# Moving the sample steps, the LayerNorm centring and the last output scaling between slots and engines of a hybrid decoder step

## What is computed

```python
# one layer; x is the residual stream, 1024 wide; 2048 prompt tokens and 16 sample tokens per core
x += 0.5 * swiglu_1(rms(x))
u, v, q, k, vB, gB, lr, gateA, gateB = split(rms(x) @ w_in)
v_n = layernorm(gelu(v)) * ln_g + ln_b                # mixer A: spatial gating in chunks of 128
y_A = gelu(u) * (tril(W_s[g]) @ v_n + b_s[g])
S_t = diag(a_t) S_{t-1} + k_t^T v_t;  o_t = q_t S_t   # mixer B: gated linear attention, 4 heads
y_B = rms_head(o) * silu(gB)
x += (sigmoid(gateA) * (y_A @ Wa) + sigmoid(gateB) * (y_B @ Wb)) @ w_out
x += 0.5 * swiglu_2(rms(x))
x += (p @ w_ple) * sigmoid(rms(x) @ w_ple_gate)
y = x * g_final * rsqrt(mean(x*x) + eps)
# every sample token owns a state S (4 x 128 x 256) that it reads, updates once and writes back
```

## Time and profile before

| | |
|---|---|
| time, median of 3 runs | 1668.87 us (1667.63 to 1670.02) |
| profiled execution, its own time | 1666.47 us |
| its span on the slowest core (core 0) | 1664.9 us |
| spans of the 8 cores | 1655.2 to 1664.9 us |
| PE busy on core 0 | 1593.3 us, 96% of the span |
| DVE, ACT, POOL busy | 676.5, 514.4, 153.5 us |

### The profile page before, as it was taken

How to read it: one execution, slowest core, us unless ns; L and a number is a source line. 1 busy time by engine, 2 the same in 40 slices (tenths; PEclk the granted TensorE clock), 3 DMA queues, 4 the chain that set the end, 5 groups by cost and what they waited for, 6 DMA issues and landing times.

```text
span 1664.9 us, 22936 instructions; the slowest of 8 cores (1655.2 to 1664.9 us)
## 1 busy us (share of the span) xinstructions
PE 1593.3 (96%) x9276; PEld 876.5 (53%) x9276; DVE 676.5 (41%) x1220; ACT 514.4 (31%) x996; POOL 153.5 (9%) x171
## 2 busy tenths in 40 slices
PE   5999999788999999999999999999999999999995
PEld 2555544344455545544666665555566666666652
DVE  3212247548445221366422225664624542222366
ACT  3112135543323112236111213575321331111144
POOL 3001000000000000000010000000000000000027
PEclk8999999889999999999999999999999999999998
DMA  9996361867746457368654424236325335325303
GB/s 161 137 158 111 41 105 32 165 162 165 153 69 97 74 78 107 62 122 127 141 82 65 70 40 68 46 46 120 52 41 87 51 51 95 58 45 84 64 1 114
DMA packets 144169, 147.74 MB, mean 89 GB/s; under 512 B 4064, under 2 KB 140016, under 8 KB 144064
## 3 DMA queue, kind: packets, MB, share of 16 engines
q0 software_dynamic: 115936, 112.01, 45.0%
q1 hardware_dynamic: 28128, 34.27, 6.8%
HBM read 240.07 MB, written 17.40 MB: 155 GB/s over the span
## 4 chain that ended last, share of the span: by engine, by line
PE 87%; DVE 4%; ACT 3%; issue 3%; DMA 2%; DVEq 0%; ACTq 0%; SPq 0%; POOLq 0%
PE ps L512 60%; PE ps L593 18%; PE ps L613 2%; PE ps L731 2%; DVE s_tsg L1677 1%; DMA s_ring<-w_ffn_in 1%; PE ps L474 1%; DMA s_ring<-w_in 1%; DVE s_xn L1315 1%; DMA s_zone<-xT 1%; PE ps L533 1%; ACT s_Sb L1164 1%; DVE s_zone L1680 1%; PE ps L760 1%; DVE s_Sf L1455 1%
## 5 line engine op out<-in xcount | busy, mean ns | idle before, releaser
L512 PE MATMUL ps<-s_xn,s_ring 128*128 128x384 bf16 (+2 forms) x5216 | 936.6, 338 | 5.4 <-ACT s_tsg L1072 1.9
L512 PEld LDWEIGHTS ps<-s_xn,s_ring 128*128 128x128 bf16 x5216 | 509.2, 98 | 405.7 <-issue 4.7
L1362 DVE TENSOR_TENSOR s_zone<-s_tsg,ps 128x384 bf16<-128x384 f32 (+2 forms) x220 | 127.8, 584 | 451.3 <-PE ps L512 431.4
L593 PE MATMUL ps<-s_zone,s_ring 128*128 128x384 bf16 (+2 forms) x1760 | 308.9, 338 | 0.0
L1050 ACT ACTIVATE s_tsg<-ps 128x384 f32<-128x384 f32 (+2 forms) x220 | 112.4, 514 | 475.3 <-PE ps L512 460.5
L593 PEld LDWEIGHTS ps<-s_zone,s_ring 128*128 128x128 bf16 x1760 | 172.2, 98 | 134.7
L1004 ACT ACTIVATE s_sqr<-s_zone 128x384 bf16<-128x384 f32 (+2 forms) x163 | 86.8, 547 | 293.2 <-DVE s_zone L1377 223.1
L512 PE MATMUL ps<-s_zone,s_ring 128*128 128x384 bf16 (+2 forms) x800 | 158.9, 339 | 0.0
L1377 DVE SCALAR_TENSOR_TENSOR s_zone<-ps,s_zone 128x384 f32<-128x384 f32 (+2 forms) x80 | 47.0, 588 | 206.4 <-PE ps L593 206.4
L1072 ACT ACTIVATE s_tsg<-ps 128x384 f32<-128x384 f32 (+2 forms) x160 | 79.7, 510 | 164.6 <-PE ps L512 163.7
L512 PEld LDWEIGHTS ps<-s_zone,s_ring 128*128 128x128 bf16 x800 | 78.5, 98 | 61.9 <-issue 1.0
(11 more groups left out here) (151 smaller groups left out, 965.8 us busy)
## 6 DMA issues: line engine op xcount, KB each, us to landing
s_ring<-w_ffn_in POOLq DMA_DIRECT2D x38, 1024.0 KB, 13.4
s_ring<-w_in POOLq DMA_DIRECT2D x24, 1024.0 KB, 13.4
s_ring<-w_ffn_out POOLq DMA_DIRECT2D x16, 1024.0 KB, 11.0
s_zone<-st SPq DMA_DIRECT2D x13, 512.0 KB, 6.4
ss_out<-s_zone SPq DMA_DIRECT2D x13, 512.0 KB, 5.9
s_ring<-w_ffn_in POOLq DMA_DIRECT2D x12, 512.0 KB, 9.2
s_ring<-w_ffn_out POOLq DMA_DIRECT2D x8, 768.0 KB, 10.5
s_zone<-xT SPq DMA_DIRECT2D x6, 768.0 KB, 10.0
```

Source lines behind the costliest of these rows:

```text
L512: ins = pe.matmul(ps[:, 0:n], piece[:, k, off:off + 128], rhs[:, k, :], start=(k == 0), stop=(k == nkc - 1))
L593: ins = pe.matmul(ps[:, 0:n], view[:, jj, c % 4 * 128:c % 4 * 128 + 128], h_v(t, j)[:, c0:c0 + n], start=(j == 0), stop=(j == JH - 1))
L1362: ins = dve.tensor_tensor(h_v(t, j)[:, c0:c0 + n], sg_of("f", f, t, j, si)[:, 0:n], bank("u", f, t, j, si)[:, 0:n], ALU.mult)
```

## The change

Four things are done together.

1. In tile 0 the sample steps in the loop run after blocks 2, 3, 4 (before: 3, 4, 5, 6), and those between the va blocks after the blocks of index 2 and 5 (before: 3). The banks of the last step of the loop go back to the queue ahead of the last iteration. A second va block is done early, in the last iteration. On DVE and ACT the step behind the loop is gone; the second k mask is made ahead of the loop.
2. In both tiles `epi_sum` of the last block moves from behind the first va block after the loop into the loop's last iteration, and its block_out banks are dropped there.
3. In both tiles DVE does `centre` of all blocks at once, behind the statistics and (tile 0) with sample steps 5, 6, 7 after every third; only `rescale` is left between the products of gb, where centre and rescale used to alternate.
4. At the end of tile 1, POOL scales segment 0 alone, and each of its scalings waits for DVE's chunk of segment 1 with the same number. DVE scales chunks 0 to 4 of segment 1 behind its chunks 3 to 7 of segment 2, then chunks 5 to 7, then all of segment 2.

```diff
-VA_EARLY = [(5,), (7, 8)]
+VA_EARLY = [(5, 6), (7, 8)]
-Y_DVE = 5
-STEPS_VA = (3,)
-STEPS_LOOP = (3, 4, 5, 6)
+STEPS_VA = (2, 5)
+STEPS_LOOP = (2, 3, 4)
...
# PE
-                if 1 <= n <= NS:
-                    bank.drop("so", n - 1, 0)
-                    bank.drop("so", n - 1, 1)
+                if 1 <= n <= NS and n != len(STEPS_LOOP):
+                    drop_so(n - 1)
...
+                    if (t, b) == (0, NBLK[0] - 1):
+                        drop_so(len(STEPS_LOOP) - 1)
                     block_out(t, b)
...
+                    else:
+                        epi_sum(t, b)
+                        bank.drop("ro", t, b, 0)
+                        bank.drop("ro", t, b, 1)
...
                     if i == len(VA_EARLY[t]):
                         for j in range(i):
                             bank.drop("va", t, ln_blocks(t)[j])
-                        epi_sum(t, NBLK[t] - 1)
-                        bank.drop("ro", t, NBLK[t] - 1, 0)
-                        bank.drop("ro", t, NBLK[t] - 1, 1)
...
# ACT
                 epi_rms(t, NBLK[t] - 1)
-                if t == 0:
-                    sample_step()
...
# DVE
                 epi_norm(t, NBLK[t] - 1)
-                if t == 0:
-                    sample_step()
...
                 if t == 0:
-                    for i in STEPS_U:
-                        sample_step()
                     dve.wait_ge(*const["lng"].at())
...
-                left = [(part, i, b) for i, b in enumerate(blocks) for part in (centre, rescale)]
+                for i, b in enumerate(blocks):
+                    centre(i, b)
+                    if t == 0 and i % 3 == 1:
+                        sample_step()
+                left = [(rescale, i, b) for i, b in enumerate(blocks)]
...
+                        if (t, si) == (1, 2) and c >= 3:
+                            scale_y(1, 1, [c - 3])
...
-            scale_y(1, last(1), range(Y_DVE))
+            scale_y(1, 1, range(5, KC))
+            scale_y(1, 2, range(KC))
...
# POOL
+            def scale_y():
+
+                n = SEGS[1][0][1]
+                pool.wait_ge(*rinvd.at("fin", 1, 0))
+                for k in range(KC):
+                    x = x_v[1][0][:, k, :]
+                    pool.wait_ge(*pled.at("x", 1, k, 1))
+                    ins = pool.tensor_tensor(x, x, rinv_tile("fin", 1, 0)[:, 0:n], ALU.mult)
+                    ins._wait_ge(*yp.at("gain", k))
+                    ins.then_inc(*yp.inc(k))
```

More of the change, by code:

```diff
@@ L737, in pe_program, with drop_so @@
             step = [0]
+            def drop_so(n):
+                bank.drop("so", n, 0)
+                bank.drop("so", n, 1)
             def sample_step():
@@ L1030, in rinv @@
                 else:
-                    tile, before = rinv_of.take((norm, t, si), yp.at(si, KC - 1) if norm == "fin" else xnd.at(norm, t, si, KC - 1))
+                    tile, before = rinv_of.take((norm, t, si), (yp.at(KC - 1) if si == 0 else yd.at(t, si, KC - 1)) if norm == "fin" else xnd.at(norm, t, si, KC - 1))
                     if before is not None:
@@ L1489, in sample_step @@
                     return
-                if n + 1 < NS:
+                if 1 <= n < NS - 1:
                     make_kmask(n + 1)
@@ L1520, in recurrence @@
                     make_kmask(0)
+                    make_kmask(1)
                 for b in range(NBLK[t]):
@@ L1798, in ple, with gain_y @@
                 load(("w", t, "pl"), wview(wple_d, 0, 1024, kc=2), 2, 1024)
[L1800 to L1813, removed]
+            def gain_y():
+                for k in range(KC):
+                    x = x_v[1][0][:, k, :]
+                    ins = pool.tensor_scalar(x, x, cols[:, C_GFIN + k:C_GFIN + k + 1], None, ALU.mult)
+                    ins._wait_ge(*squared.at("fin", 1, 0, k))
+                    ins.then_inc(*yp.inc("gain", k))
+            def scale_y():
+                n = SEGS[1][0][1]
+                pool.wait_ge(*rinvd.at("fin", 1, 0))
+                for k in range(KC):
+                    x = x_v[1][0][:, k, :]
+                    pool.wait_ge(*pled.at("x", 1, k, 1))
+                    ins = pool.tensor_tensor(x, x, rinv_tile("fin", 1, 0)[:, 0:n], ALU.mult)
+                    ins._wait_ge(*yp.at("gain", k))
+                    ins.then_inc(*yp.inc(k))
             for t in range(NT):
@@ L1829, in pool_program @@
             pool.wait_ge(*ccols.at())
[L1830 to L1833, removed]
+            gain_y()
+            scale_y()
         def sp_program(sp):
@@ L1845, in store_y @@
                 c0 += TFIRST[t]
-                sp.wait_ge(*(yd.at(0, si, KC - 1) if t == 0 else yp.at(si, KC - 1)))
+                sp.wait_ge(*(yp.at(KC - 1) if (t, si) == (1, 0) else yd.at(t, si, KC - 1)))
                 sp.dma_start(out=yv[:, :, c0:c0 + n], in_=x_v[t][si]).then_inc(*ys[t, si].inc())
@@ L1887, in sp_program @@
             for i in range(4):
-                for k in (2 * i, 2 * i + 1):
-                    sp.wait_ge(*(yd.at(1, 2, k) if k < Y_DVE else yp.at(2, k)))
+                sp.wait_ge(*yd.at(1, 2, 2 * i + 1))
                 sp.dma_start(out=yv[:, 2 * i:2 * i + 2, c0:c0 + n], in_=x_v[1][2][:, 2 * i:2 * i + 2, :]).then_inc(*ys[1, 2].inc(i))
```

## The result

The changed kernel takes 1650.23 us (median of 3 runs, 1649.12 to 1652.99) where before takes 1668.87: ratio 0.9896, interval 0.9881 to 0.9911. The medians differ by 18.6 us, the forecast was 19.6. Its profiled execution took 1649.12 us, with a span of 1647.6 us on its slowest core, core 3. Some executions, whatever the kernel, before included, take 3 to 18% longer with a lower TensorE clock on one half of the cores or on both; all medians and ratios here leave these out.

A forecast was written before the change was run, and what follows sets the result against it. PE was taken to bound the kernel, busy 96% of the span, so edits pay only where PE waits or behind its last matmul. -15.0 - 0.7 - 3.9 = -19.6 us takes the median 1668.9 to 1649.3; range 1643 to 1657.

The forecast's parts named there:

- The mixer of tile 0: Tile 0's mixer up to gate A's second pair: PE's bank, mask and sg waits go, -15.0 us.
- The new waits: PE's waits in tile 0's va (1.7 us) and ahead of two u projections (0.6 and 1.3 us), 3.6 in total.
- step 10: Sample step near the end of gb in tile 0's mixer: PE's 0.9 us wait there stays.
- the lower bound of the mixer: Tile 0's mixer: only the idle time up to the u projection goes, new waits doubled: -6 us.
- first rival: Tile 0's mixer: ACT's sample casts become the bound, new waits 10 us, sg waits half back; total -11.6, 1657; 18%.
- Tile 1: Tile 1's mixer: PE's 0.7 us wait for a gelu goes, -0.7 us (0 to -1).
- The end: After PE's last matmul: DVE's 7.79 us lock-out goes, the stores then decide, -3.9 us.
- bound of -7: At the end: -7 us if the stores overlap, the last pair alone ending at 1657.8.
- second rival: At the end: DVE is held all the same, by another cause or POOL's paced scalings; total about -13, 1656; 10%.
- The third: Tile 0's mixer, 319 to 392 us: PE's low clock stays, kernel slower, a whole low mixer +45 us; 5%.
- the fourth: Waits only move: the 7.9 us reappear in va and the stores hide the rest, within 0.2%; 3%.
- The sum: Whole kernel: -15.0 - 0.7 - 3.9 = -19.6 us, from the median 1668.9 to 1649.3.

The follow-up runs named there:

- later casts: Changed kernel with ACT's sample-step casts one gelu later, in va and under u: 1646.14 us; with segment 1's y also stored in pairs: 1642.29 us.
- part 4 alone: Kernel before with only the new end (the diff's lines on y: scalings, stores and their waits): 1661.83 us, ratio 0.9977.
- with pairs: Changed kernel with segment 1's y stored in four pairs of chunks as scalings end, instead of one store: 1644.90 us, ratio 0.9873.
- The row with four scalings: Kernel before with each POOL scaling of segment 1 waiting for DVE's same-numbered chunk of segment 2: 1663.37 us, ratio 0.9980.

## Why the prediction was right

**The mixer of tile 0.** With the 1.2 us taken off, the milestones stand as computed:

| | predicted | measured |
|---|---|---|
| end of epi_sum(6) | 325.2 | 325.4 |
| end of the first u projection | 340.3 | 340.5 |
| sg | 383.9 to 388.6 | 384.2 to 388.8 |
| gate A's second pair | 392.1 | 392.6 |

So the stage gave 14.5 us between these two cores, where 15.0 were forecast. The new waits were 1.2 (forecast 1.7), 0.6 (0.6) and 1.6 (1.3), and step 10's 0.4 where 0.9 was to stay. The block_out(6) start, forecast at 319.1, came at 320.2 behind 1.7 us of head norm. What made up for it is the clock: the full level was back at 323.8 (325.0 less the 1.2) where 324.5 was taken. The low level returns for a few microseconds at gate A's first pair, which takes 2.85 us, as it did in before (the prediction did not list it, and it cancels).

That the milestones agree to half a microsecond is in part luck. The cores run the same program, and the stretch takes 97.4 to 100.6 us on the eight of this profile; core 3 with 98.5 is near their median of 98.6, and core 0 of before, from which the schedule was computed, is the longest of its eight (113.1, median 111.7). Between the medians the profile gives 13.1 us, and over all runs of either mixer 12.7 (112.3 to 99.6). So the mechanism held, and the size of -15.0 is 2 us too large for the typical core.

The causes behind the steps are shown by the runs, not only argued: the bank wait is 4.2 us if `epi_sum` is late, the steps' old places bring 5.2 us of waiting and a lower clock, the sg waits come back with the centring under gb. What the prediction did not say is that the three parts overlap: undone one at a time (part 1, 2, 3) they are worth 2.2, 2.2 and 2.8 us by the times, and 2.7, 2.3 and 3.7 by the stretch, while all three are worth 14. Any two of them keep over 11 of it.

Two bounds of the prediction do not follow from its own terms. The waits of the earlier trace rows add 11.3 us, so with 7.2 of new waits the lower bound of the mixer is -4.1 and not -6; and the first rival's terms (-6.6, -0.7, -3.9) add to -11.2 and not -11.6. Neither moves the forecast.

**The first rival** (ACT's sample casts become the bound, 1657) named the right resource at the wrong size: a cast waits 3.83 us for DVE and holds three gelus (ACT's timeline), where one waited 3.17 in the earlier trace rows, and PE waits 3.4 us for gelus on core 3 (1.9 to 3.7 over the cores), not 10.

```profile
335.11 1.06 ACT L1181 ACTIVATE s_psn<-s_zone 128x1024 bf16<-128x1024 f32 x1 [3.83 <-DVE s_zone L1500]
336.07 1.55 ACT L1240 ACTIVATE s_zone<-ps 128x512 f32<-128x512 f32 x3
```

The runs with later casts, where none of these waits is left on any core, show that they came from there.

**Tile 1.** The 0.7 us wait is gone, and comes back when part 2 is undone; no gelu stands in PE's waits from 1100 to 1200 us (largest: 0.8 for a state cast, 0.4 for a mask). It is too small for the time of a run to show.

**The end.** Forecast -3.9, measured -3.8 (part 4 alone) and, between the two profiles, 43.4 to 39.0 us from POOL's first scaling of y to the end (1621.48 to 1664.9, 1608.60 to 1647.6), so -4.4 (-4.2 between the medians of the cores). The steps held: sums never above 1.06 us, scalings at 0.61, the stores decide. The term that was a little off is the rate: the 3.15 MB of two segments went at some 370 GB/s, 8.5 us in place of 9.2. The 340 of the earlier trace rows was misread as a full rate: the last 0.2 us of that window had no data, and the two whole microseconds before, 1661 to 1663, stand at 366 and 367. The bound of -7 "if the stores overlap" was within reach: with pairs 3.0 us more were had.

**The second rival** (DVE is held all the same, 1656) is out: neither the paced nor the unpaced scalings of segment 0 hold DVE for longer than one of them. The row with four scalings confirms the reading of the earlier trace rows, that the hold lasts as long as POOL's run without a gap. What ended it in the changed kernel is that POOL no longer scales segment 1 beside DVE's chunks of segment 2; the gaps alone end most of it too. The pacing of segment 0 is not needed, and costs 0.9 us of the end. The Trainium skill, SBUF — State Buffer, section "Who interferes with whom", lets the second instruction wait until the first one's whole instruction ends. The trace agrees where scalings are apart, 1.06 us for one, and in segment 0's run, 0.78 to 0.97; it differs in segment 1's, 3.99 us for four and 7.79 for eight.

**The third and the fourth** (the clock stays low; waits only move) did not come. Part of the fourth is true all the same: with part 1 or part 2 undone, waits stand early and the later ones vanish, at a cost of only 2 to 3 us.

**The sum.** Stage by stage the two profiles give -14.5 - 0.7 - 4.4 = -19.6 us, which is the forecast's sum by luck: the mixer came out short and the end long by the same 0.5, on one core of each profile. Their spans differ by 17.3 only. 1.2 of the rest is core 3's lag ahead of the mixer, and 1.3 is a wait of PE for a load of w_in between the mixer and the end, which is 1.0 us on core 0 of before and 2.3 here (PE's waits, 410 to 1600 us):

```profile
PE ps L510 <- DMA s_ring<-w_in: 2.3, 1, 2.3
```

This wait is absent on core 0 of the changed kernel, 2.2 on its core 4, and 1.4 and 1.7 on cores 3 and 4 of before, so it goes with the core at least as much as with the kernel. Between the medians of the cores the stages give 12.7 + 0.7 + 4.2 = 17.6 us, and the times 17.3 (by the ratio) to 18.6 (by the medians). So the forecast of 19.6 is 1 to 2 us high, most likely in the mixer; a difference of this size is within what the times can't tell.

## What to carry to other kernels

Where matmuls take their banks from a queue, find for each long wait which `drop` put that bank there: moving a drop ahead of a block can be worth more than making the waited-for engine faster. Check for each cast or load that waits for a third engine whether something that frees a bank is queued behind it; moving such an instruction one place later changed two lines and gave 3.8 us. At the end of a kernel count the bytes that are left when the last operand is ready, and store in pieces as they come: 3.0 us here by the traces, 3.8 by the times. Read a stretch on every core before calling a forecast of it exact to a few tenths: here the cores of one execution differ by 3 us in one stage. Do not add up the worth of edits that were each tried by undoing them alone, when they all feed one queue.

## What the hardware showed that was not expected

- A DVE addition beside a run of POOL multiplications can be held for the whole run when these follow each other without a gap: 7.79 us beside eight in 7.65, 3.99 beside four in 3.85, 1.06 beside one of 1.00. But the eight of segment 0, 9.28 us, also without a gap, let DVE's additions in at 0.78 to 0.97 us each; POOL's own instructions then take 1.31 us each, against 0.99 in the held case. Operation, shapes and types are the same. What differs in the traces is when the addition starts. In the 13 profiles and all their cores, the 24 additions that were held for a run began 0.27 to 0.29 us after a POOL instruction had begun; the 160 that were let in during a run began 0.43 us or more after. In both cases an addition ends 0.41 to 0.42 us after the POOL instruction that it waited out. No run varied the start by itself, so that it decides is not shown.
- Once the waits were gone, parts of 2 to 4 us each were worth 14 together, partly through the clock. In the window 318 to 345 us the clocks of the cores are 0.56 to 0.80 in before (median 0.71), 0.68 to 0.87 without part 1 (0.72), 0.81 to 0.87 without part 2 (0.85), 0.87 to 0.96 without part 3 (0.93), 0.87 to 0.96 in the changed kernel (0.94) and 0.94 to 1.00 with the later casts (0.95). The waits of that window are shorter in the same order, from 7.9 us in before, through 3.8 to 4.2 in the next two, to at most 1.7. How much of the 14 us is the clock and how much the waits was not separated.
